# Low parts of the input projection's weight granules: formed on VectorE instead of GpSimd

## What is computed

```python
h = rms_norm(x, norm1_w)
y = h @ w_in                      # 1024 x 3852: all inputs of three head groups
fq, fk, fv, ff, rq, rk, rv, rg, gq, gk, gv, gz, ga, gb = split_columns(y)
# FoX attention (fq, fk, fv, ff), retention (rq, rk, rv, rg), gated delta rule (gq ... gb),
# the last with a causal convolution of width 4 and silu on gq, gk, gv
x = x + concat(o_fox, o_ret, o_gdn) @ w_out
x = x + hier_moe(rms_norm(x, norm2_w))   # 32 experts, top 2 of one group of 8
return rms_norm(x, final_norm_w)
```

## Time and profile before

| | |
|---|---|
| time, median of 3 runs | 681.57 us (679.59 to 682.13) |
| the profiled execution | 681.12 us, of which the span of the trace is 679.3 us |
| TensorE busy | 583.0 us (86% of the span) |
| VectorE busy | 242.7 us (36%) |
| ScalarE busy | 199.0 us (29%) |
| GpSimd busy | 173.0 us (25%) |
| input projection, first to last matmul of L686 | about 20.5 to 269.4 us |

### The profile page before, as it was taken

The page is one execution under the profiler, slowest core; times in us unless marked ns, Lnnn a source line. Parts: engine busy times, 40 slices in busy tenths (PEclk is TensorE's granted clock), DMA queues, the critical chain, the costliest instruction groups (busy, mean ns, idle before and its releaser), DMA issues.

```text
span 679.3 us, 11973 instructions
## 1 busy us (share of the span) xinstructions
PE 583.0 (86%) x4912; PEld 454.1 (67%) x4912; DVE 242.7 (36%) x618; ACT 199.0 (29%) x428; POOL 173.0 (25%) x114
## 2 busy tenths in 40 slices
PE   2999999779999899988859993899999997877782
PEld 1997777579999788766649993565665664444441
DVE  4225343453213611365671116233233232212217
ACT  6434444422224252533522332011111111111113
POOL 1244334233266522400123320111211211111003
PEclk9999999989999999989969996699999999999997
DMA  8566864211221111000049939899999999999975
GB/s 322 172 168 189 52 241 121 64 32 33 64 62 38 41 51 64 1 1 1 1 126 353 409 103 387 328 383 419 420 421 417 419 420 419 420 420 419 419 296 211
DMA packets 53543, 151.64 MB, mean 223 GB/s; under 512 B 12543, under 2 KB 34863, under 8 KB 40944
## 3 DMA queue, kind: packets, MB, share of 16 engines
q1 hardware_dynamic: 48864, 142.69, 56.8%
q0 software_dynamic: 4560, 8.15, 3.2%
q10 hardware_dynamic: 64, 0.02, 0.0%
HBM read 142.70 MB, written 16.27 MB: 234 GB/s over the span
## 4 chain that ended last, share of the span: by engine, by line
PE 57%; SPq 14%; DMA 12%; DVE 9%; ACT 3%; issue 3%; POOL 2%; ACTq 0%; POOLq 0%; DVEq 0%
PE bank L686 26%; PE bank L708 8%; SPq L579 6%; PE bank L958 4%; DMA w<-in_expert_w_dram 4%; SPq L585 4%; PE bank L993 4%; PE bank L973 4%; SPq L582 3%; DMA cbd<-small 3%; DMA raw<-in_w_in_dram 3%; PE bank L928 2%; PE bank L942 1%; PE bank L862 1%; DMA yd<-oy,dst 1%
## 5 line engine op out<-in xcount | busy, mean ns | idle before, releaser
L1283 POOL TENSOR_TENSOR wlo<-raw,whi 128x1024 fp32r<-128x1024 f32 (+1 forms) x38 | 91.1, 2398 | 194.8 <-ACT whi L1016 194.8
L686 PE MATMUL bank<-whi,hHi 128*128 128x256 f32 (+1 forms) x352 | 101.3, 288 | 3.1 <-issue 1.7
L686 PE MATMUL bank<-wlo,hHi 128*128 128x256 f32 (+1 forms) x352 | 99.9, 284 | 0.0
L686 PE MATMUL bank<-whi,hLo 128*128 128x256 f32 (+1 forms) x352 | 99.7, 283 | 0.0
L1016 ACT ACTIVATE whi<-raw 128x1024 fp32r<-128x1024 f32 (+1 forms) x38 | 40.3, 1060 | 116.0 <-PE bank L686 108.4
L958 PE MATMUL bank<-w,xT 128*64 128x256 f32 x512 | 60.8, 392 | 11.3 <-issue 8.2
L686 PEld LDWEIGHTS bank<-whi,hHi 128*128 128x128 f32 x352 | 67.0, 190 | 4.2 <-issue 2.0
L686 PEld LDWEIGHTS bank<-whi,hLo 128*128 128x128 f32 x352 | 67.1, 191 | 0.0
L686 PEld LDWEIGHTS bank<-wlo,hHi 128*128 128x128 f32 x352 | 67.0, 190 | 0.0
L958 PEld LDWEIGHTS bank<-w,xT 128*64 128x64 f32 x512 | 39.5, 141 | 37.4 <-issue 21.5
L973 PE MATMUL bank<-w,xT 128*64 128x256 f32 x512 | 58.3, 380 | 7.1 <-DMA w<-in_expert_w_dram 7.1
(11 more groups left out here) (321 smaller groups left out, 878.2 us busy)
## 6 DMA issues: line engine op xcount, KB each, us to landing
w<-in_expert_w_dram SPq DMA_DIRECT2D x48, 2048.0 KB, 28.3
raw<-in_w_in_dram SPq DMA_DIRECT2D x24, 512.0 KB, 4.0
yd<-zt SPq DMA_DIRECT2D x8, 512.0 KB, 5.1
raw<-in_w_out_dram SPq DMA_DIRECT2D x8, 512.0 KB, 4.3
yt<-yd SPq DMA_DIRECT2D x4, 1024.0 KB, 9.0
raw<-in_w_in_dram SPq DMA_DIRECT2D x6, 520.0 KB, 7.3
X<-in_x_dram SPq DMA_DIRECT2D x4, 512.0 KB, 6.5
x<-in_x_dram SPq DMA_DIRECT2D x4, 512.0 KB, 5.0
```

The lines of the kernel that those rows point to most:

```text
L686: m = pe.matmul(o, l, r, start=(kc == 0 and i == 0), stop=(kc == KC - 1 and i == 2), skip_group_check=True)
L1283: pool.tensor_tensor(wlo[g % 2][:, :, 0:w], raw[g % 3][:, :, 0:w], whi[g % 2][:, :, 0:w].bitcast(F32), ALU.subtract).then_inc(wlo_done, 1)
```

## The change

The function `weight_low` for the input projection moves from GpSimd's program to VectorE's, with the same operands and the same semaphore. VectorE forms the low parts of granules 0 and 1 behind all eight instructions of hLo, and that of granule g + 2 at the head of its tasks after granule g. GpSimd keeps its `prep` and `rotary` tasks in the same order and waits once, behind them, until 32 low parts are formed. It keeps its own `weight_low` for the output projection's granules 32 to 37.

```diff
@@ gpsimd
-            weight_low(0)
-            weight_low(1)
-
             def task(k):
...
             for g in range(GR_IN):
-                weight_low(g + 2)
                 for k in AFTER[g]:
                     task(k)
+            pool.wait_ge(wlo_done, GR_IN + 2)
 
             pool.wait_ge(silu2_done, 1)
@@ vector
+            def weight_low(g):
+                w = 256 if g >= GR_IN else GROUPS[g // 2][3]
+                dve.wait_ge(whi_done, g + 1)
+                dve.tensor_tensor(wlo[g % 2][:, :, 0:w], raw[g % 3][:, :, 0:w], whi[g % 2][:, :, 0:w].bitcast(F32),
+                                  ALU.subtract).then_inc(wlo_done, 1)
+
+            weight_low(0)
+            weight_low(1)
...
             for g in range(GR_IN):
+                weight_low(g + 2)
                 for k in AFTER[g]:
                     task(k)
```

## The result

The changed kernel took 700.97 us in the median of 4 runs (697.03 to 702.08), against 681.85 (679.59 to 682.26, 4 runs) of the kernel before beside it: a ratio of 1.0279 (95%: 1.0248 to 1.031), so 19.1 us slower. The forecast was 699.8. The profiled execution took 702.08 us with a span of 700.3, which is 21.0 more than the span of before.

The account below looks back on a forecast made before the run. TensorE's matmuls bound the first 283 us, so what makes TensorE wait counts. Terms 2.9 + 0.15 + 0.7 + 0.9 + 10.2 + 3.4 = 18.25 us on the median 681.57 gave 699.8 us, range 695.5 to 703.5 (8 in 10).

Parts of the forecast that it names:

- start: Projection's first matmul: granule 0's low part follows the last hLo, so TensorE starts at 23.33 instead of 20.45, +2.9 us.
- granules 2 to 15, with 8 and 13: Granule 8's later low part delays column stores and granule 13's load; with the taps behind 13's low part, +0.15 us.
- taps: Convolution taps start 0.69 us later behind a low part; granule 16 waits for two of their banks, +0.7 us.
- prep 0: During granule 17, Dm stands behind granule 19's low part, delaying ScalarE's exponential and TensorE, which waits on it: +0.9 us.
- levels 0 and 1 (0.25 + 1.35) with rotary (3.4): Behind granules 18 and 19: low part ahead of Y costs 0.25 and 1.35 us, plus 3.4 us for rotary's collisions.
- levels from 2 on: Steps 20 to 29: Xp later by 0.85 to 0.87 us (even), 1.34 to 1.41 (odd), 1.0 at 23, nothing at 25.
- the mechanism and the largest term: In the levels VectorE waits for whi and forms the low part before Y, delaying Xp: +10.2 us in sum.
- the price: A low part on VectorE: 1.22 us, or 1.24 for 1040 elements, bounds 1.1 and 2.4 us.
- rotary: Behind granules 18 and 19: rotary slides forward on GpSimd and VectorE loses the shared port, +3.4 us, bounds 0 and 3.4.
- the rival of the clock: Level 0 and one or two more half-empty TensorE stretches lower its clock: 701.5 to 703.2 us, chance 0.22.
- granule 13: Its load comes 1.2 us later, its low part is 1.17 quicker; TensorE's start stays within 0.1 us.
- the rival with a gain: TensorE's 4.9 and 0.91 us waits come from GpSimd's queue and vanish, Y having slack: 678.7 us, chance 0.04.

Follow-up runs that it names:

- after again: The changed kernel, unchanged, run and profiled a second time on one chip with the kernel before: 703.96 us, ratio 1.0308.
- before again: The kernel before, unchanged, profiled a second time on the same chip as the runs beside it: 681.02 us in one run.
- e1: Against the changed kernel: in the eleven levels VectorE turns Y first and forms the low part after it; 692.93 us, ratio 1.0131.
- e4: Against the kernel before: VectorE also waits for whi ahead of its tasks, while GpSimd still forms the low parts; 691.6 us, ratio 1.0118.
- e3: Against the changed kernel: from granule 18 on GpSimd waits for the low part, so rotary runs where it ran before; 701.18 us, ratio 1.0287.
- e7: Against the changed kernel: rotary held back as in e3 and loads of granules 13 and 14 ahead as in e5; 696.44 us, ratio 1.0194.
- e2: Against the changed kernel: VectorE forms granule 0's low part ahead of hLo; 700.71 us, ratio 1.0269.
- e5: Against the changed kernel: SP issues the loads of granules 13 and 14 before waiting for the column stores; 697.55 us, ratio 1.0223.
- e8: Against e5: TensorE runs 20 matmuls, later overwritten, while waiting for the first low part; 697.23 us, ratio 1.0194.
- e9: Against the kernel before: GpSimd forms only the first 128 columns of each input granule's low part, the rest zero; 679.47 us, ratio 0.9948.

## Why the prediction was right, term by term

| term | forecast | after, first pair of profiles | after again less before again |
|---|---|---|---|
| start | 2.9 | 5.7 | 2.4 |
| granules 2 to 15, with 8 and 13 | 0.15 | 0.0 | 0.3 |
| taps | 0.7 | 0.6 | 0.6 |
| prep 0 | 0.9 | 1.5 | 0.5 |
| levels 0 and 1 (0.25 + 1.35) with rotary (3.4) | 5.0 | 5.0 | 4.6 |
| levels from 2 on | 8.6 | 9.7 | 8.2 |
| after the projection | 0 | -1.5 | 0.2 |
| sum | 18.25 | 21.0 | 16.7 |

The two right columns are differences within the table of distances (prep 0 is whi 18 to whi 20, levels from 2 on are whi 22 to whi 31 and a last level of 1.4). The median moved by 19.1, between the two.

**Right: the mechanism and the largest term.** Ym starts behind the low part and TensorE waits for it at ten places. The forecast had even steps of about 0.86 and odd ones of about 1.37; the same-chip pair shows 0.85, 1.36, 0.81 and 0.76 behind granules 20 to 23, nothing at 24 and 25, then 0.83, 1.41, 0.80 and 1.37. e1 takes this away in full from level 1 on, and e4 shows that it is the instruction's length and not the wait for whi.

**Right: the price.** 1.22 to 1.23 us, estimated at 1.22.

**Right in sum, wrong in its parts: rotary.** VectorE does not win the port, and e3 and e7 take away 3.5 and 3.0 us, forecast 3.4. But level 0 cost 1.4 and 0.9 us in the two pairs where 2.75 was forecast. The collisions themselves had nearly the size forecast: the three products of prep 1 were lengthened by 2.0 in all (forecast 2.4) and the low part by 0.9 (forecast 1.0). What failed is the path. The forecast had the low part start 2.6 us behind the end of whi (163.4 against 160.8); it started 0.4 behind (168.96 against 168.55), and at once in the second execution. TensorE was itself late there, since part of granule 18 ran at half clock behind prep 0, and most of what the products lost fell into that time. Level 1's Xp came 2.2 us later (forecast 2.25), and then TensorE ran at half clock: Xp took 0.83 longer and granule 20 began slowly, together 1.4. Level 1 cost 3.6 to 3.7 us in all five traces of after's form with rotary not held (after, after again, e2, e5, e8), and 1.3 with rotary held (e3, e7). So 1.4 us of what was measured are the clock, which the sum did not have, and they stood in for 1.4 that the collision did not cost at level 0. The match to 0.1 is luck.

**Partly true: the rival of the clock.** I put it at 0.22. Level 1 brought it in both executions (0.58) and in e2, e5 and e8 as well, the start in one (2.3 us), level 5 in one (0.62, 1.5 us). The spans of after's two executions differ by 4.5 us, of which 2.8 stand at whi 2 and 1.5 at level 5; between these the table shows ups and downs of about 1 us. The error was to treat the clock as a case apart. It is a term of 1.4 us at level 1, with up to 4 more that change from execution to execution.

**Right, within what can be read: prep 0.** Dm started at 152.39, that is 146.15 beside the 6.24 by which all was late (whi 18), forecast 146.28, and the longest wait for Nm grew from 3.6 to 4.4 us, forecast 0.9 more. The rest is clock: behind this gap the mean granted clock was 0.50 for 4 us in after, and the same in the second execution of before, but 0.76 and 0.81 in the first one (148 to 156 us):

```profile
158.00:162.00 4.00, 4.00 (x21) 4.00 (x21) 2.48 (x10) 1.15 (x2) 0.21 (x1) 0.50 0.02 6
```

```profile
152.00:156.00 4.00, 4.00 (x19) 4.00 (x20) 2.80 (x11) 1.12 (x2) 0.20 (x1) 0.50 0.02 4
```

The first fence is after, the second before again. That before's own step there was 1.5 us larger in its second execution makes this term readable to some 1 us and no better; in the other traces of after's form the step from whi 18 to whi 20 was 0.0 (e1) to 2.2 us (e5).

**Underrated: granule 13.** I had +0.15 with TensorE's start "within 0.1". In the traces of after's form the wait there was 0.86, 2.01, 4.60, 5.07 and 5.22 us, in those of before 0.91 and 1.74. The three longest are all of one chip, as is e4's 3.28, and behind them granule 13 ran in part at 1.2 GHz, for 1.4 to 2.6 us more. Is it the change's doing? With the loads ahead in both kernels the difference of the medians is 697.55 - 679.67 = 17.9 us, and the ratios (1.0223 and 0.9951) differ by 2.7%, as those of after and before do (2.8%). So on the median the term is small, as forecast; but it is what spreads the times, and in the traces it outweighed e2's and e3's gains. These two kernels were timed on different occasions, so 17.9 is good to perhaps 2 us.

**Refuted: the rival with a gain.** It needed VectorE's Y to end before UT did. That held nowhere in the levels. What a quicker low part can bring is at most e9's 0.5%, and its row in the table shows none of it at the start or in the levels.

## What to carry to other kernels

Ask of a moved instruction not how busy the new engine is but what stands behind it in that engine's order and who waits for that: 1.2 us on an engine busy 36% made TensorE wait up to 2.2 us at each of ten places, and nothing once it stood behind the instruction that TensorE wanted. An instruction taken out of an engine's program also lets go what it held back there, and the work that slides forward may meet another engine. When an experiment shows less than its trace promises, look through the whole trace for a loss elsewhere, here a small store whose time varies by 4 us and that the loads on its queue stood behind, and repeat the unchanged kernel where the experiment ran.

## What was not expected of the hardware

- **Matmuls at half speed with a recorded clock of 1.00.** From 24 to 28 us of after the row of the stretch says 1.00, while 260 columns took 0.216 us from start to start, which is 1.2 GHz. In e7 it is the same; in e1, e3 and e5 equally slow matmuls of granule 0 stand under 0.50. Behind level 1 the same 0.42 us stand under 0.58. The Trainium skill, "TensorE: Matmul & The Clock Gate", section "Seeing it yourself", warns that the clock's trace events have been seen to be unreliable; the row at the start agrees. The spacing of equal matmuls is the safer reading.
- **The port holds GpSimd up, too.** Where VectorE's low part got in between two rotary instructions, the GpSimd instruction beside it took 2.13 and 2.07 us instead of 1.08 to 1.28. The Trainium skill, "SBUF — State Buffer", section "Who interferes with whom", describes the shared port as an exclusive lock: the instruction that is issued first holds it and the other side waits. The trace agrees with that taken in turns: the low part of 168.96 ended 1.08 us after GpSimd's instruction of 168.71 did, and the GpSimd instruction begun at 170.07 ended 1.13 us after the low part.
- **The column stores' time varies.** From SP's issue of them to the first load behind them it took 20.4 and 21.4 us in before, 20.9 and 21.5 in after, 23.3 in e4, 22.4 in e9, and 24.1, 24.5 and 23.6 in e1, e2 and e3. The four longest are all from one chip; whether that or something else sets it was not found.
